# A recurrent mixer's last gates: turned pairs multiplied with gate and norm before a weight split instead of behind it, on VectorE and ScalarE

## What is computed

```python
def mlstm_mixer(x, w_in, b_if, conv_w, norm_g, w_out):
    proj = x @ w_in
    qk, v, o, if_pre = jnp.split(proj, [...], axis=-1)
    qk = jax.nn.silu(causal_depthwise_conv_2(qk, conv_w))
    q, k = jnp.split(qk, 2, axis=-1)
    ...
    h = mlstm_chunkwise(q, k.reshape(B, T, H, dk), v.reshape(B, T, H, dv), i_log, f_log)
    h = head_rms(h).reshape(B, T, H * dv) * norm_g.astype(F32)
    h = (h * jax.nn.sigmoid(o.astype(F32))).astype(x.dtype)
    return h @ w_out
```

## Time and profile before

| | us |
|---|---|
| median of three executions | 2827.66 |
| lowest and highest of them | 2824.71, 2828.87 |
| profiled execution, its own time | 2817.83 |
| profiled execution, its span | 2816.0 |
| TensorE (PE) busy | 2709.7 |
| VectorE (DVE) busy | 1761.0 |
| ScalarE (ACT) busy | 1418.7 |
| GpSimd (POOL) busy | 138.0 |

### The profile page before, as it was taken

One profiled execution on the slowest core, in us unless ns is written; L12 is line 12 of the kernel. 1 busy time (PEld: TensorE's weight loads), 2 busy tenths in 40 slices (PEclk: granted clock), 3 DMA queues, 4 the chain that ended last, 5 costly groups with the idle time before them and its releaser, 6 DMA issues.

```text
span 2816.0 us, 47880 instructions
## 1 busy us (share of the span) xinstructions
PE 2709.7 (96%) x19782; PEld 2443.1 (87%) x19782; DVE 1761.0 (63%) x2133; ACT 1418.7 (50%) x1872; POOL 138.0 (5%) x206
## 2 busy tenths in 40 slices
PE   7899999899999999999998999999999999999999
PEld 7789999788888888879897888889988888898887
DVE  5555788765556566579655556566556666555655
ACT  5544577544555455457224455454344454445544
POOL 3000000000000000000301000000000000000000
PEclk9989999999999999999999999999999999999999
DMA  7164899555535555544203555555445555553553
GB/s 205 45 217 166 278 353 353 194 190 193 158 106 182 187 175 191 190 136 149 78 4 124 190 194 182 190 168 190 147 156 196 193 172 192 182 157 107 186 191 123
DMA packets 371293, 491.97 MB, mean 175 GB/s; under 512 B 12313, under 2 KB 331377, under 8 KB 371121
## 3 DMA queue, kind: packets, MB, share of 16 engines
q1 hardware_dynamic: 367968, 479.51, 50.9%
q0 software_dynamic: 2576, 7.97, 1.0%
q10 hardware_dynamic: 576, 1.98, 0.2%
HBM read 488.38 MB, written 1.05 MB: 174 GB/s over the span
## 4 chain that ended last, share of the span: by engine, by line
PE 89%; DVE 5%; ACT 3%; issue 1%; POOL 1%; DMA 0%; ACTq 0%; POOLq 0%; DVEq 0%
PE bank L351 21%; PE bank L350 11%; PE bank L330 9%; PE bank L331 9%; PE bank L332 9%; PE acc L330 7%; PE acc L332 7%; PE acc L331 7%; PE bank L2876 1%; ACT w_hi L295 1%; PE acc L604 1%; PE bank L2853 1%; DVE X L509 1%; DVE act_both L530 1%; PE bank L2864 1%
## 5 line engine op out<-in xcount | busy, mean ns | idle before, releaser
L300 DVE TENSOR_TENSOR w_lo<-raw,w_hi 128x2048 fp32r<-128x2048 f32 x360 | 823.9, 2292 | 503.6 <-ACT w_hi L295 502.8
L295 ACT ACTIVATE w_hi<-raw 128x2048 fp32r<-128x2048 f32 x360 | 688.0, 1912 | 267.6 <-PE acc L332 229.4
L351 PE MATMUL bank<-act_both,w_hi 128*128 128x512 f32 x2560 | 654.7, 392 | 0.0
L351 PEld LDWEIGHTS bank<-act_both,w_hi 128*128 128x128 f32 x2560 | 465.2, 189 | 82.8
L350 PEld LDWEIGHTS bank<-act_both,w_lo 128*128 128x128 f32 x2560 | 349.1, 190 | 25.0
L330 PE MATMUL acc<-w_hi,mix_hi 128*128 128x512 f32 x928 | 364.0, 392 | 4.4 <-ACT att_probs L1175 2.2
L332 PE MATMUL acc<-w_hi,mix_lo 128*128 128x512 f32 x928 | 362.0, 390 | 0.0
L331 PE MATMUL acc<-w_lo,mix_hi 128*128 128x512 f32 x928 | 361.7, 390 | 0.0
L350 PE MATMUL bank<-act_both,w_lo 128*128 128x256 f32 x2560 | 356.8, 282 | 0.0
L738 ACT ACTIVATE scratch<-bank 128x256 f32<-128x256 f32 x320 | 122.4, 385 | 429.1 <-PE bank L351 422.6
L330 PE MATMUL bank<-act_both,w_hi 128*128 128x256 f32 x1032 | 298.1, 289 | 14.5 <-DVEq L2290 8.0
(11 more groups left out here) (516 smaller groups left out, 3867.1 us busy)
## 6 DMA issues: line engine op xcount, KB each, us to landing
raw<-in_ffn_w_gu SPq DMA_DIRECT2D x176, 1024.0 KB, 5.0
raw<-in_ffn_w_down SPq DMA_DIRECT2D x88, 1024.0 KB, 4.8
raw<-in_ml_w_in SPq DMA_DIRECT2D x24, 1024.0 KB, 5.2
raw<-in_rt_w_in SPq DMA_DIRECT2D x24, 1024.0 KB, 5.2
raw<-in_w_up SPq DMA_DIRECT2D x20, 1024.0 KB, 6.9
raw<-in_w_gate SPq DMA_DIRECT2D x19, 1024.0 KB, 6.5
raw<-in_w_down SPq DMA_DIRECT2D x18, 1024.0 KB, 6.0
moe_raw<-in_w_down SPq DMA_DIRECT2D x14, 1024.0 KB, 6.0
```

The source lines that it names most:

```text
L295: act.activation(w_hi[0:rows, slot, 0:size], raw[0:rows, slot, 0:size], ACT.Copy).then_inc(hi_made, 1)
L300: dve.tensor_tensor(w_lo[0:rows, slot, 0:size], raw[0:rows, slot, 0:size], w_hi[0:rows, slot, 0:size].bitcast(F32), ALU.subtract).then_inc ...
L351: return pe.matmul(bank[b][:, :], w_hi[:, slot, w], act_both[:, k, :], start=k == 0, stop=k == KT - 1)
```

## The change

On VectorE, `ahead("o", 2)`, the low part of weight panel 13, stands no longer ahead of `out(0)`, but behind `low(1)`; `out(1)` stands ahead of `low(0)`, and `out(2)` ahead of `low(1)`. On ScalarE, the high part of the same panel is split off from `projected("o", 2)` and stands behind `high(1)`. The same instructions are issued, and no wait is taken away or added; the list of `ml_dve` names the steps in the new order, since each step is known by its count. The lists of TensorE, GpSimd and SyncE stay as they are.

```diff
--- before.py
+++ after.py
@@ -1996,7 +1996,7 @@
         ML_PAN = {(x, j): 4 * i + j for i, x in enumerate("vqo") for j in range(4)}
         ml_dve = Steps("ml_dve", ["cleared", "z", "e1", "g", "conv0", "nM", "conv1", "m", "conv2", "conv3"]
                        + [f"S{h}" for h in range(4)] + ["rd", "scaled2", "scaled3"]
-                       + [x for j in range(4) for x in (f"out{j}", f"low{j}")])
+                       + ["out0", "out1", "low0", "out2", "low1", "low2", "out3", "low3"])
         ml_act = Steps("ml_act", ["tanh", "exp", "ln", "em"] + [f"D{h}" for h in range(4)] + [f"silu{j}" for j in range(4)]
                        + ["ad"] + [f"squares{h}" for h in range(4)] + ["scaled0", "scaled1"] + [f"high{j}" for j in range(4)])
         ml_pool = Steps("ml_pool", ["rs"])
@@ -2120,6 +2120,10 @@
             def read(last, *key):
                 last.then_inc(evacuated[N[key] % BANKS], 1)
 
+            def ahead(x, j):
+                q = c.p + ML_PAN[x, j] + RING
+                act_split(act, q % RING, loads(q), E[x, j])
+
             def projected(x, j):
                 b = got(x, j)
                 pair = b[:, :].rearrange("p (m t) -> p m t", m=2)
@@ -2132,8 +2136,8 @@
                 else:
                     last = act.activation(ml_o[:, 2 * j:2 * j + 2, :], pair, ACT.Sigmoid)
                 read(last, x, j)
-                q = c.p + ML_PAN[x, j] + RING
-                act_split(act, q % RING, loads(q), E[x, j])
+                if (x, j) != ("o", 2):
+                    ahead(x, j)
 
             def decays(h):
                 b = got("D", h)
@@ -2187,6 +2191,7 @@
                 ml_act.done(act.activation(mix_hi[:, 2 * j:2 * j + 2, :], ml_o[:, 2 * j:2 * j + 2, :], ACT.Copy), f"high{j}", r)
             high(0)
             high(1)
+            ahead("o", 2)
             high(2)
             projected("o", 3)
             high(3)
@@ -2277,7 +2282,6 @@
                     last = dve.tensor_scalar(scratch[:, t, h * ML_DV:(h + 1) * ML_DV], acc[h][:, t * T:t * T + T],
                                              ml_rs[:, t, h:h + 1], None, ALU.mult)
                 ml_dve.done(last, f"scaled{h}", r)
-            ahead("o", 2)
 
             def out(j):
                 wait_evacuated(dve, N["o", j])
@@ -2295,9 +2299,13 @@
                 ml_act.wait(dve, f"high{j}", r)
                 ml_dve.done(dve.tensor_tensor(mix_lo[:, k, :], ml_o[:, k, :], mix_hi[:, k, :].bitcast(F32),
                                               ALU.subtract), f"low{j}", r)
-            for j in range(3):
-                out(j)
-                low(j)
+            out(0)
+            out(1)
+            low(0)
+            out(2)
+            low(1)
+            ahead("o", 2)
+            low(2)
             out(3)
             low(3)
             ahead("o", 3)
```

## The result

The changed kernel took 2809.91 us in the median of four executions (2806.09 to 2813.86), the kernel before 2826.18 on the same chip (four, 2823.54 to 2828.87). The ratio is 0.9948, with an interval of 0.9934 to 0.9961: 14.7 us less, between 11.0 and 18.7 (the two medians by themselves are 16.3 apart). Forecast was 2816.4 for the median, 11.3 us less, in a range of 2810 to 2823. The forecast gain lies inside the interval of the measured one, at its lower end. One execution of the kernel before, timed beside the experiments, took 3086.94 us with a clock of 0.819; it is a slow one and counts in no ratio.

What follows compares the result with a forecast made beforehand. TensorE's own work was taken as the bound, 89% of the chain. Gap 7.9 plus clock in o3 3.4 made 11.3 us, from the median 2827.66 to 2816.4, range 2810 to 2823.

Steps and rivals of the forecast that it cites:

- The place and the mechanism: In each mixer TensorE idles 4.0 us ahead of o3, waiting for out(0), which stands behind panel 13's low part on VectorE.
- The gap: TensorE's idle time between turns and o3 shrinks to 0.05 us in each mixer, a gain of 7.9 us.
- The clock in o3: Without the gap o3 runs at full clock, 5.85 us in both mixers; gain 3.4 us, 2 to 5 in other executions.
- Panel 13: Its low part, moved later on VectorE, is ready level with o3's end, 5.5 us before TensorE wants it; no cost.
- the rival of the wait that comes back: Panel 13's low part comes too late for TensorE; 2827.7 if the whole gain is lost; chance 0.08.
- low stretches behind 866 us: Lower-clock stretches after the first mixer; the prediction fails if they grow by more than 3 us in sum.
- The slower rival, the load of panel 16: SyncE's load of panel 16 lands too late for ScalarE's split, delaying the next norm; 2833.3 us; chance 0.04.
- Nothing behind o3 changed: From o3's end to the norm behind the mixer all distances stay as before, out(3) not delayed; cost 0.
- The first rival: TensorE's idle time ahead of o3 goes but the clock term does not; 2819.8 us; chance 0.15.

Runs made afterwards that it cites:

- e1_out0_only: Kernel before, with only VectorE's out(0) moved ahead of the low part of panel 13, all else unchanged; ratio 0.9947 to the kernel before, 15.0 us less.
- e3_gap3: Changed kernel with three unused products on VectorE between its wait for turn 0 and out(0), a 2.06 us TensorE gap; ratio 0.9976 to the kernel before.

## Why the prediction was right

**The place and the mechanism** were as told: o3 stood for out(0), and out(0) behind a weight panel that nobody yet needed. `e1_out0_only` shows that this one place in VectorE's order is the whole effect.

**The gap.** Predicted 7.9, measured 8.0 (8.1 in the sum of TensorE's waits). The 0.05 that I left per mixer wasn't there. One link was wrong without a price: I had out(0) wait for the gate of o2 and begin 0.85 us behind the first turn. By the kernel, out(0) waits for the gate of o0, long done, and only out(2) needs that of o2. It began at 0.72 (828.66 - 827.94), held by turn 0, ahead of the end of o2's gate (828.14 + 0.60).

**The clock in o3** is the term that was mis-sized: 3.4 predicted, 4.6 in the mean of four traces of the kernel before, with 3.5 in the one that I had. The step that failed is reading both places of one trace as if they were typical. The prediction said that the term could lie between 2 and 5, which held, but then took the trace's value; it also put the median's 9.8 us above the profiled execution down to nothing that the change touches, while part of these 9.8 us was this term (stretches of 26.9 us in the execution of 2817.83 us, 28.1 to 28.8 in those of 2825 and 2826). That is 1.2 us of the 1.5 between 11.3 and the located 12.8. The rest up to the timed 13.3 to 15.5 us lies within the intervals.

**Panel 13** was ready level with o3's end and started 4.6 us behind the gate of o2 (833.38 and 828.74), both as written, and its reserve was 5.5 us as worked out. With it goes the rival of the wait that comes back. One sign that the prediction named as its failure, low stretches behind 866 us that grow by more than 3 us, is met by the first pair of traces, which differ by 3.8 us between the two stretches. The seven traces of the two kernels show it to be chance: there the kernel before ranges over 4.9 us and the changed one over 6.7, around nearly the same mean (1747.8 and 1747.0). The slower rival, the load of panel 16, showed nothing even when the load was released 6 us later still.

**Nothing behind o3 changed**: out(3) and the gate of o3 touch without delay, and the gaps of TensorE up to the next norm are the 2.0 us of before.

**The first rival**, the idle goes and the clock stays, is refuted by o3 at clock 1.00 in all places without a gap, six in the changed kernel, and by `e3_gap3`, in which a gap alone brings the loss back.

**By the Trainium skill**, "TensorE: Matmul & The Clock Gate", Part 1, the moment of the clock's fall is not tied to the kernel. The traces agree: in the eight places of the kernel before, all with the same 4.0 us of gap, the clock fell between 4.1 and 5.4 us behind the first turn, and the loss in o3 was 1.2 to 2.7 us.

## What to carry to other kernels

Where an engine prepares operands for later work and also releases what TensorE wants next, look in its list for the long preparation that stands ahead of the short release; its reserve is the distance from when it is ready to when it is used. Here it had some 14 us (ready at 828.99, used at 842.7 in the first mixer) and still has 5.5 after the move, which took away a gap of 4. A gap of TensorE costs more than its length as long as the clock answers to it: here 4.0 us cost 6.3. And the clock's share must come from several traces or several places: a stretch that bounds the change on both sides repeats to 0.02 us where whole spans of one kernel differ by 11.

## What the runs showed of the hardware that was not expected

The lower clock need not begin in the gap. With a gap of 2.06 us it began 1.1 us after TensorE was at work again in the first mixer and some 0.3 us after it in the second, and took 1.5 us from o3 in both. Counted from the first turn, the fall came 4.1 to 5.8 us behind it in all twelve places with a gap, whether the gap was 2.06, 4.0 or 4.23 us long. The 1.8 us of turns, small matmuls, stand ahead of every gap here, and turns with no gap behind them brought no fall. So these traces can't tell whether the turns count as rest along with the gap, and 2.06 us is not shown to be enough behind other work.

The loss doesn't grow in step with the gap either: 1.5 us each for 2.06 us, 2.7 and 1.3 for 4.23, 1.2 to 2.7 for 4.0. The part of a low stretch that lies in the gap takes nothing from o3: in the first trace's second mixer the clock fell 1.8 us ahead of the gap's end. At full clock o3 needs 5.83 us.
